# Three attentions in one kernel: in each step TensorE does the weighted sums of the part four steps back ahead of the scores of the newest part

## The reference

```python
logits = einsum(q, k) * HEAD_DIM ** -0.5        # masked
p = softmax(logits, axis=-1)
o = einsum(p, v)
```

## Time and profile before

| | |
|---|---|
| median of 3 runs | 2438.68 us (2436.54 to 2439.32) |
| profiled execution, its own time | 2441.7 us |
| its span | 2439.9 us |
| TensorE, matmuls | 2308.2 us, 95% of the span |
| VectorE | 1843.9 us, 76% |
| ScalarE | 1328.6 us, 54% |
| granted TensorE clock, mean | 0.955 |

### The profile page before, as it was taken

One profiled execution on the slowest core, in us unless ns is written; L12 is line 12 of the kernel. 1 busy time (PEld: TensorE's weight loads), 2 busy tenths in 40 slices (PEclk: granted clock), 3 DMA queues, 4 the chain that ended last, 5 costly groups with the idle time before them and its releaser, 6 DMA issues.

```text
span 2439.9 us, 30442 instructions
## 1 busy us (share of the span) xinstructions
PE 2308.2 (95%) x12485; PEld 1896.3 (78%) x12485; DVE 1843.9 (76%) x2245; ACT 1328.6 (54%) x1345; POOL 34.1 (1%) x62
## 2 busy tenths in 40 slices
PE   7989999998899999999999999998889999888999
PEld 4756999656688888888888888876778997656998
DVE  4756564686788989898989898976647888765887
ACT  3333543453477777777777777764444343465432
POOL 1000000000000000000000000000000000000000
PEclk9988999998999999999999999997879999879999
DMA  9634655671599999999999999993415554302553
GB/s 335 226 140 160 224 183 185 207 257 70 168 364 369 369 345 356 368 363 347 355 375 363 341 362 375 363 346 100 138 48 176 185 190 144 122 1 87 183 190 104
DMA packets 281283, 584.43 MB, mean 240 GB/s; under 512 B 12030, under 2 KB 86892, under 8 KB 281008
## 3 DMA queue, kind: packets, MB, share of 16 engines
q1 hardware_dynamic: 277600, 572.33, 66.6%
q0 software_dynamic: 3536, 10.08, 1.3%
HBM read 581.32 MB, written 1.05 MB: 239 GB/s over the span
## 4 chain that ended last, share of the span: by engine, by line
PE 86%; DVE 7%; ACT 4%; DMA 2%; issue 1%; POOL 0%; DVEq 0%; ACTq 0%; POOLq 0%
PE ps L1287 24%; PE ps L1288 24%; PE ps L1289 24%; PE ps L1340 3%; DVE w_lo L1915 2%; PE ps L1419 2%; PE ps L1404 1%; PE ps L1675 1%; ACT arena L1001 1%; PE ps L1442 1%; PE ps L1531 1%; DMA raw<-in_w_ada 1%; DVE arena L2137 1%; PE ps L1692 1%; DVE arena L1932 1%
## 5 line engine op out<-in xcount | busy, mean ns | idle before, releaser
L904 ACT ACTIVATE w_hi<-raw 128x2048 fp32r<-128x2048 f32 x500 | 948.5, 1906 | 432.8 <-PE ps L1289 315.3
L1915 DVE TENSOR_TENSOR w_lo<-raw,w_hi 128x2048 fp32r<-128x2048 f32 x500 | 1117.9, 2272 | 32.3 <-ACT w_hi L904 29.2
L1287 PE MATMUL ps<-w_hi,xT_hi 128*128 128x512 f32 (+4 forms) x1184 | 464.3, 392 | 16.3 <-DVE xT_lo L1966 6.5
L1289 PE MATMUL ps<-w_hi,xT_lo 128*128 128x512 f32 (+4 forms) x1184 | 458.7, 387 | 0.0
L1288 PE MATMUL ps<-w_lo,xT_hi 128*128 128x512 f32 (+4 forms) x1184 | 458.6, 387 | 0.0
L1287 PE MATMUL ps<-xT_hi,w_hi 128*128 128x256 f32 x1056 | 299.7, 284 | 4.0 <-DVE xT_lo L1966 4.0
L1288 PE MATMUL ps<-xT_lo,w_hi 128*128 128x256 f32 x1056 | 299.6, 284 | 0.0
L1289 PE MATMUL ps<-xT_hi,w_lo 128*128 128x256 f32 x1056 | 299.5, 284 | 0.0
L1287 PE MATMUL ps<-w_hi,aT_hi 128*128 128x512 f32 (+1 forms) x744 | 287.4, 386 | 2.2 <-DVE aT_lo L2277 1.4
L1288 PE MATMUL ps<-w_lo,aT_hi 128*128 128x512 f32 (+1 forms) x744 | 287.2, 386 | 0.0
L1289 PE MATMUL ps<-w_hi,aT_lo 128*128 128x512 f32 (+1 forms) x744 | 286.7, 385 | 0.0
(11 more groups left out here) (368 smaller groups left out, 2380.4 us busy)
## 6 DMA issues: line engine op xcount, KB each, us to landing
raw<-in_moe_w_gate SPq DMA_DIRECT2D x112, 1024.0 KB, 5.7
raw<-in_moe_w_up SPq DMA_DIRECT2D x112, 1024.0 KB, 5.4
raw<-in_moe_w_down SPq DMA_DIRECT2D x112, 1024.0 KB, 5.8
raw<-in_w_ada SPq DMA_DIRECT2D x48, 1024.0 KB, 6.0
raw<-in_f_w_up SPq DMA_DIRECT2D x44, 1024.0 KB, 5.0
raw<-in_f_w_down SPq DMA_DIRECT2D x22, 1024.0 KB, 5.0
raw<-in_w_in SPq DMA_DIRECT2D x20, 1024.0 KB, 6.6
raw<-in_a_w_in SPq DMA_DIRECT2D x12, 1024.0 KB, 5.1
```

What stands on the lines that cost most here:

```text
L904: act.activation(w_hi[:, k % HI, 0:size], raw[:, r, 0:size], ACT.Copy).then_inc(ring.w_hi_ready, 1)
L1287: pe.matmul(out_, lh, rh, start=start, stop=False)
L1289: return pe.matmul(out_, ll, rh, start=False, stop=stop)
L1915: dve.tensor_tensor(w_lo[:, k % RAW, 0:size], raw[:, k % RAW, 0:size], w_hi[:, k % HI, 0:size].bitcast(F32), ALU.subtract).then_inc(ring.w ...
```

## The change

In TensorE's loop over the steps the two `if` statements of the scores and the sums change places. In step k the order is then T(k-3), O(k-4), S(k). No wait, no count and no operand differs, and no other engine's program does.

```diff
                 for k in range(n + 4):
                     if at.lead <= k - 3 < n:
                         transposed(k - 3)
+                    if 0 <= k - 4 < n and at.parts[k - 4][0] != "heads":
+                        sums(k - 4)
                     if k < n and at.parts[k][0] != "heads":
                         scores(k)
-                    if 0 <= k - 4 < n and at.parts[k - 4][0] != "heads":
-                        sums(k - 4)
                 pe.wait_ge(att_taken, at.outs(n - 1))
```

## The result

| | before | changed |
|---|---|---|
| median | 2437.61 us (4 runs, 2434.07 to 2439.32) | 2457.56 us (4 runs, 2457.18 to 2458.45) |
| ratio | | 1.0077, 95% interval 1.0055 to 1.0098 |
| profiled execution | 2441.7 us, span 2439.9 | 2458.45 us, span 2456.6 |
| mean granted clock of it | 0.955 | 0.951 |

The changed kernel is slower, as forecast, but by 20.0 us where 10.0 were forecast, and its time is 1.6 us above the range. Later sets of runs gave half of that; the experiments come to it.

A forecast was written before the change was run, and what follows sets the result against it. The prediction took a two-step loop through the scores as the bound, with sums mostly beside it. Forgetting +4.3 and native +5.7 gave +10.0 us on the 2438.68 median: 2448.7 us (+0.41%), range 2443 to 2456.

The forecast's parts named there:

- no new wait of O for the taken output: Sums moved earlier: their waits are met already, price 0 to 0.4 us a step, taken as 0; a new wait would refute.
- S later: Both long attentions: scores start after the sums, delaying transposes that wait for the copy by the whole sum, less slack; +10.0 us.
- the native sum: Native sparse attention: delays followed through seven binding waits of transposes, 6.12 less overlaps gives 5.6, taken as +5.7 us.
- the step on the clock: Both long attentions: TensorE's clock levels kept as they were despite 10 us more idleness; no clock cost counted.
- the third rival: Slower by more: longer idle keeps TensorE at the low clock in one forgetting and two native steps; +6.8, 2455.5 us; chance 0.18.
- step 13: Forgetting attention: the step that the clock rival expected to stay at the low level, costing 3.0 us.
- the lines given for it: Profile signs: VectorE's score waits 70 us or more, attentions 70.8 and 98.7 us, T(8) about 2.7 later, copy waits growing like stretches.

The follow-up runs named there:

- experiments 2 to 5: Against the kernel before: new order per attention, 1.0021 and 1.0028; in nine or thirteen steps, 1.0067 and 1.0013; two sums doubled, 1.0022; scores ahead of transposes, 0.9945.
- the 132 executions: 104 executions of the kernel before and 28 of the changed kernel, each with its mean clock; at the same mean clock the change costs 10.3 us.
- the two halves: New order in only the forgetting or only the native sparse attention, against the kernel before: 1.0021 and 1.0028.
- The two sets of 12: The changed kernel run again unchanged, 12 runs each, against the kernel before: 1.004 (2448.47 us) and 1.0043 (2453.84 us).
- the two kernels kept busy: Old and new order, each with two unread matmuls before transposes in the long attentions' steps with scores, against the kernel before: 0.9966 and 1.0009.
- exp. 1: The kernel before run once more without edit, against itself in the same rounds: 0.999, median 2436.6 us of 12 runs.
- native only: New order only in the native sparse attention, against the kernel before: 1.0028.
- the thirteen steps: New order only in the 13 moved steps not named as binding, old order elsewhere, against the kernel before: 1.0013.
- changed x3: The changed kernel's three sets, against the kernel before: 1.0077 (4 runs), 1.004 and 1.0043 (12 runs each).
- forgetting only: New order only in the forgetting attention, against the kernel before: 1.0021.
- the nine steps: New order only in steps 9, 13 (forgetting) and 7, 10, 13, 17, 21, 23, 26 (native), against the kernel before: 1.0067, 2455.73 us.
- sums twice: Old order with O(5) and O(9) of the forgetting attention done both ahead of and behind the scores, against the kernel before: 1.0022.
- scores first: Scores ahead of transposes, then sums (save step 14 of the forgetting attention), against the kernel before: 0.9945, median 2424.44 us.
- kept busy, old order: Old order plus two unread matmuls before transposes in the long attentions' steps with scores, against the kernel before: 0.9966, median 2433.78 us.
- kept busy, new order: New order plus two unread matmuls before transposes in the long attentions' steps with scores, against the kernel before: 1.0009, median 2444.36 us.

## Why the prediction was right or wrong

**The mechanism of the order was right.** S sits on a loop of two steps and O beside it; what is moved in front of S is paid. The two small attentions were untouched (17.0 us from the first S of the second to the transposes behind it, in both profiles), no new wait of O for the taken output appeared, and the waits for O, 7.0 us, stayed. *S later*, step by step: the loop's 4.78 us behind S(9) and S(13) did not change, and experiments 2 to 5 show that what stands in front of S is what counts.

**The loss at equal clock was near the forecast.** 10.0 us were forecast, 4.3 and 5.7 for the two attentions; at equal mean clock the 132 executions give 10.3, and the two halves 4.4 and 6.1. The two sets of 12 gave 1.0040 and 1.0043. Part of the agreement is luck: the native sum came out by another path (below), T(8) came 1.4 us later for the 2.7 forecast, the ratios contain a clock loss that I did not count, and so does the 10.6 us between the two kernels kept busy.

**What failed is the step on the clock: "I keep the levels as they were."** In the forgetting attention the order's own share is O(5) and O(9) in front of S, 4.26 us. The rest of the 7.6 us is clock: from T(8) to the end of S(13) it was 6.64 us before (1778.56 to 1785.20) and 12.82 after (1782.72 to 1795.54). Of these 6.18 us the O(9) would have cost 1.52 at full clock; 4.66 are T(8), T(9), O(8), S(12), T(10) and most of O(9) at 1.2 GHz instead of 2.4. S(9), at full this time (2.02 for 3.62), gave 1.6 back, so that T(8) came 1.44 us later, counted from the attention's start (35.22 for 33.78), and not 2.7. In all five profiles with O(5) moved ahead of S(9) and no added matmuls, the stretch from T(8) to the end of S(13) took 12.1 to 12.8 us and S(9) 1.99 to 2.02; in the four with the old order in these steps they took 6.6 to 6.7 and 3.62. The profiles of the variants show that these steps are no chance (T(9) has eight transposes, T(10) too):

```
profile                          idle before T(8)   T(9) us   T(10) us
before, exp. 1, native only,
  the thirteen steps             1.11 to 1.16       1.09-1.10   1.04-1.07
changed x3, forgetting only,
  the nine steps                 3.90               1.97        1.91-1.92
sums twice                       2.27               1.29        1.92
scores first                     1.49               1.05        1.04
kept busy, old order             2.27               1.37        1.04
kept busy, new order             3.90               1.92        1.04
```

In five of five profiles with O(5) ahead of S(9) the engine had been idle for 3.90 us and the steps behind ran at 1.2 GHz; in four of four with it behind, after 1.11 to 1.16 us, they ran at 2.4. Up to T(9) only the place of O(5) divides these groups: the native-only kernel and that of the thirteen steps have moved sums elsewhere, and the nine steps lack thirteen of the moves. Of the two kept busy, the added matmuls brought the full clock back within the next step. So the fall of the clock there is a consequence of the change. That the gap of 1.11 us becomes 3.9 could have been read off; that the gap is what lowers the clock is the nearest reading, but not shown, because S(9) at the full clock ahead of it always comes with the longer gap, and with the sums done twice the clock fell after a gap of 2.27. I reckoned what O costs where it goes and not what it leaves behind. This is the third rival, though not at its place: it named step 13, where S(13) ran at full as before (1.99 for 1.89), and the low steps are 11 and 12 and the T and O of 13. Its price of 3.0 is near the net of this profile, 3.3 us (7.6 - 4.3); I had given it 0.18. In the other profiles of the new order the whole attention took 70.9 to 74.0 us, with the same low steps: what they cost is partly made up elsewhere in some of them.

In the native attention the sum held, but not its path. Waits in the changed kernel's timeline of PE: T(6), T(9), T(12), T(16), T(20), T(22), T(25).

```profile
2156.47 1.09 PE L1404 MATMUL ps<-const,arena 128*128 128x128 f32 x8 [2.41 <-ACT arena L1022]
2166.35 0.61 PE L1404 MATMUL ps<-const,arena 128*15 128x128 f32 x4 [1.15 <-ACT arena L1015]
2177.16 0.61 PE L1404 MATMUL ps<-const,arena 128*15 128x128 f32 x4 [0.95 <-ACT arena L1022]
2191.57 0.61 PE L1404 MATMUL ps<-const,arena 128*15 128x128 f32 x4 [0.72 <-ACT arena L1015]
2204.67 1.09 PE L1404 MATMUL ps<-const,arena 128*128 128x128 f32 x8 [1.47 <-ACT arena L1022]
2211.45 0.61 PE L1404 MATMUL ps<-const,arena 128*15 128x128 f32 x4 [0.26 <-ACT arena L1022]
2221.66 0.61 PE L1404 MATMUL ps<-const,arena 128*15 128x128 f32 x4 [1.02 <-ACT arena L1022]
```

Less the 10.33 us by which this attention began later, the delays are 0.59, -0.98, 1.30, 2.72, 3.08, 4.29 and 6.24 us, against 0.80, 1.82, 2.47, 3.70, 4.82, 5.47 and 6.12 in the prediction. T(9) and T(16), which had followed without idle time, now wait. At T(16) the slack was spent as reckoned: the copy that it waits for came 2.8 us later. At T(9) it was not: that copy came no later than before (0.1 us earlier), and TensorE was early, because what it does ahead of T(9) ran at half clock before and at full after, T(6) above all (1.97 and 1.09 us). From T(9) on the loss is 7.2 us for the 4.3 forecast, and no row here says which steps made up the difference.

**The range missed because it took too small a scatter of the runs.** I saw three runs within 2.8 us and a profile 3.0 above them, and read the scatter from that. The same program's executions range from 2430 to 2452 us, and 0.001 of mean clock is 1.6 us. The 20.0 us of the result are 12.1 of the change over all executions, 2.7 from four runs of the kernel before that were below its mean (2437.6 for 2440.3), and 5.2 from four of the changed kernel above its mean (2457.56 for 2452.4), all at a clock of 0.950 to 0.952. So of the 10 us by which the forecast missed, 2 lie in the change and 8 in which executions the four were. The 12.1 in turn are 10.3 at equal mean clock and 1.8 from a lower one (0.9543 for 0.9552). Why four executions in a row had the low clock, when later sets ran from 0.950 to 0.959, stays open. Open too is how the 12.1 divide into delay and the clock that the change itself costs: a mean clock over the whole run cannot tell the low steps behind T(8) from chance elsewhere, and the sums of the stretches in the profiles (three or four of each order) differ by 14.9 us, more than the medians do; the profiled executions with the new order were slow ones of their sets.

By the lines given for it, the prediction was right on VectorE's waits (72.5 for "70 or more") and wrong on the stretches (74.1 and 99.7 for 70.8 and 98.7), on T(8) (1.4 us later for 2.7), and on TensorE's waits for copies, which grew by 8.2 us where the stretches grew by 14.0; the added idle time came before T(8) and S(14), behind copies of heads, and in VectorE's wait.

## What to carry to other kernels

In a pipeline over several engines, follow the loop from the engine's work through the others and back, and put on the engine's queue first what the loop waits for; work beside the loop was free behind S here and cost its duration in front, though nothing is added; and where it leaves a gap, look at what the granted clock does behind it. Where an engine's clock is granted by its activity, ask how much the executions of one program scatter before a difference of half a percent is read, and compare runs at the same mean clock as well, knowing that this takes out what the change itself costs through the clock. The loop that explains a loss also names the opposite edit: here scores ahead of the transposes gained 0.55%.

## What was not expected of the hardware

The granted clock of an unchanged stretch differs from execution to execution: the forgetting attention before was granted 0.67 in one and 0.73 in another, and took 66.6 and 63.1 us. The 56 added matmuls whose results nobody reads made the old order faster by 0.34% (0.17 to 0.5), with the clock in the two attentions at 0.89 and 0.92; the Trainium skill ("TensorE: Matmul & The Clock Gate", Part 1) says that activity releases the slow level, and this run agrees.
